# Fifteen instead of eleven pairs of value units as seven block products, in a two-layer hybrid decoder trunk

## The reference

```python
eidx = jnp.take_along_axis(cidx, pos, axis=-1)          # 16 of 16384 experts for each of 8 heads
g = jax.nn.softmax(sc, axis=-1)
act = jax.nn.gelu(jnp.einsum('bchkd,bcd->bchk', u[eidx], hb).astype(jnp.float32))
return jnp.einsum('bchk,bchkd->bcd', (g * act).astype(hb.dtype), v[eidx])
```

## Time and profile before

| | |
|---|---|
| time, median of 3 runs | 2419.32 us (2418.03 to 2420.98) |
| time of the profiled execution | 2415.21 us |
| its span, first to last instruction | 2413.4 us |
| mean granted clock of TensorE | 0.999 |
| PE busy | 2386.7 us, 99% |
| PEld (weight loads) busy | 2215.5 us, 92% |
| DVE busy | 1885.1 us, 78% |
| ACT busy | 1437.1 us, 60% |
| POOL busy | 790.1 us, 33% |

### The profile page before, as it was taken

The page is one execution under the profiler, slowest core; times in us unless marked ns, Lnnn a source line. Parts: engine busy times, 40 slices in busy tenths (PEclk is TensorE's granted clock), DMA queues, the critical chain, the costliest instruction groups (busy, mean ns, idle before and its releaser), DMA issues.

```text
span 2413.4 us, 43665 instructions
## 1 busy us (share of the span) xinstructions
PE 2386.7 (99%) x17465; PEld 2215.5 (92%) x17465; DVE 1885.1 (78%) x3186; ACT 1437.1 (60%) x2115; POOL 790.1 (33%) x452
## 2 busy tenths in 40 slices
PE   9999999999999999999999999999999999999999
PEld 8999999999999988888799999999999999888887
DVE  7988777498489975888778886865974899768886
ACT  5586664444677764655455966644446777555553
POOL 0011410288899820000000113003888988100000
PEclk9999999999999999999999999999999999999999
DMA  7533345355544455666555333453555444566654
GB/s 262 215 123 123 122 141 189 135 184 185 177 162 160 158 201 192 211 208 214 183 186 207 133 123 112 152 185 137 184 184 175 158 160 162 196 198 211 200 183 157
DMA packets 103016, 419.26 MB, mean 174 GB/s; under 512 B 11552, under 2 KB 12064, under 8 KB 85920
## 3 DMA queue, kind: packets, MB, share of 16 engines
q1 hardware_dynamic: 102816, 416.47, 50.7%
HBM read 415.38 MB, written 1.05 MB: 173 GB/s over the span
## 4 chain that ended last, share of the span: by engine, by line
PE 85%; DVE 6%; ACT 3%; DMA 3%; issue 2%; POOL 1%; SPq 0%; DVEq 0%; ACTq 0%
PE banks L2278 20%; PE banks L407 18%; PE banks L408 18%; PE banks L409 18%; PE banks L2260 3%; DMA xr<-in_xstream 2%; PE banks L2294 1%; PE banks L2295 1%; PE banks L2293 1%; DVE ring_lo L382 1%; PE banks L867 1%; ACT xr_hi L1871 1%; DVE xr_lo L1876 1%; POOL xr_lo L1876 1%; PE banks L754 1%
## 5 line engine op out<-in xcount | busy, mean ns | idle before, releaser
L1871 ACT ACTIVATE xr_hi<-xr 128x1024 fp32r<-128x1024 f32 x468 | 493.8, 1056 | 437.7 <-DMA xr<-in_xstream 437.3
L1876 POOL TENSOR_TENSOR xr_lo<-xr,xr_hi 128x1024 fp32r<-128x1024 f32 x256 | 619.9, 2426 | 388.7 <-ACT xr_hi L1871 388.3
L407 PE MATMUL banks<-featH,xr_hi 128*128 128x256 f32 x2048 | 576.1, 281 | 1.1 <-POOL xr_lo L1876 1.1
L408 PE MATMUL banks<-featL,xr_hi 128*128 128x256 f32 x2048 | 575.7, 281 | 0.0
L409 PE MATMUL banks<-featH,xr_lo 128*128 128x256 f32 x2048 | 575.3, 281 | 0.0
L407 PEld LDWEIGHTS banks<-featH,xr_hi 128*128 128x128 f32 x2048 | 385.7, 188 | 1.9 <-POOL xr_lo L1876 1.0
L409 PEld LDWEIGHTS banks<-featH,xr_lo 128*128 128x128 f32 x2048 | 386.1, 189 | 0.0
L408 PEld LDWEIGHTS banks<-featL,xr_hi 128*128 128x128 f32 x2048 | 385.9, 188 | 0.0
L1876 DVE TENSOR_TENSOR xr_lo<-xr,xr_hi 128x1024 fp32r<-128x1024 f32 x212 | 259.3, 1223 | 159.1 <-ACT xr_hi L1871 157.9
L407 PE MATMUL banks<-featH,ring_hi 128*128 128x256 f32 x1232 | 351.0, 285 | 2.2 <-DVE ring_lo L382 1.5
L408 PE MATMUL banks<-featL,ring_hi 128*128 128x256 f32 x1232 | 346.2, 281 | 0.0
(11 more groups left out here) (416 smaller groups left out, 4629.9 us busy)
## 6 DMA issues: line engine op xcount, KB each, us to landing
xr<-in_xstream SPq DMA_DIRECT2D x468, 512.0 KB, 3.3
ring<-in_wstream SPq DMA_DIRECT2D x128, 1024.0 KB, 4.9
b_raw<-in_xstream SPq DMA_DIRECT2D x88, 256.0 KB, 3.6
smw<-in_small SPq DMA_DIRECT2D x4, 617.0 KB, 9.2
first<-in_wstream SPq DMA_DIRECT2D x4, 512.0 KB, 5.5
first<-in_wstream SPq DMA_DIRECT2D x2, 1024.0 KB, 7.9
subk<-in_subkeys SPq DMA_DIRECT2D x2, 1024.0 KB, 7.7
x<-in_x SPq DMA_DIRECT2D x2, 512.0 KB, 5.6
```

The source lines that it names most:

```text
L407: PE.matmul(o, s_hi_lo[0], m_hi_lo[0], start=first, stop=False)
L408: PE.matmul(o, s_hi_lo[0], m_hi_lo[1], start=False, stop=False)
L1871: A.activation(xr_hi[:, m % XR], xr[:, m % XR], ACT.Copy).then_inc(s_xhi, 1)
L1876: (PO if m < NKEY else V).tensor_tensor(xr_lo[:, m % XR], xr[:, m % XR], xr_hi[:, m % XR].bitcast(F32), ALU.subtract).then_inc(s_xlo_pool ...
```

## The change

`SEVEN` names 15 pairs instead of 11. The first three stay where they were (7, 15, 23); behind them the pairs are alternately three and two apart instead of four. The sevens then stand ahead of plain units 14, 28, 42, 46, 48, 52, 54, 58, 60, 64, 66, 70, 72, 76 and 78 of 98. Between two of them lie 4 or 2 plain units, where 6 lay before. The steps in `lead` are set anew, so that for the alternating sevens the first sums stand two units ahead of the seven before, the last sums, `sums_high` and `b_low` one unit ahead of it, and all the rest at it. For the first three sevens `b_low`, `a_high`, `a_sums` and `a_sums_high` come one step later. Four loads of the second buffer set are issued in two steps instead of four, and the next layer's first splits stand at units 120 and 124 (ACT) and 122 and 126 (DVE). The loads of the next layer are tied to the last sevens and move with them.

```diff
--- before.py
+++ after.py
@@ -110,8 +110,8 @@
-SEVEN = (7, 15, 23, 27, 31, 35, 39, 43, 47, 51, 55)
-SEVEN_SET = (0, 0, 0, 1, 0, 1, 0, 1, 0, 1, 0)
+SEVEN = (7, 15, 23, 26, 28, 31, 33, 36, 38, 41, 43, 46, 48, 51, 53)
+SEVEN_SET = (0, 0, 0, 1, 0, 1, 0, 1, 0, 1, 0, 1, 0, 1, 0)
 PLAIN = tuple(i for i in range(NKEY) if i // 2 not in SEVEN)
 ONE_BY_ONE = len(PLAIN)
 SEVEN_AT = tuple(2 * r - 2 * j for j, r in enumerate(SEVEN))
@@ -2098,17 +2098,17 @@
                 OTHER_FREE = sum(i < 42 for i in PLAIN)
                 OTHER_AFTER = sum(2 * r < 42 for r in SEVEN)
-                def lead(j, units, later=0):
-                    return SEVEN_AT[j] - units if SHARED[j] else SEVEN_AT[j - 1] - 1 + later
-                B_HIGH = FIRST_SUMS = tuple(lead(j, 11) for j in range(NS))
-                LAST_SUMS = tuple(lead(j, 10) for j in range(NS))
-                SUMS_HIGH = B_LOW = tuple(lead(j, 9, 1) for j in range(NS))
-                A_HIGH = A_SUMS = tuple(lead(j, 8, 1) for j in range(NS))
-                A_SUMS_HIGH = tuple(lead(j, 7, 1) for j in range(NS))
-                SUMS_LOW = tuple(lead(j, 6, 1) for j in range(NS))
-                A_LOW = tuple(lead(j, 4, 3) for j in range(NS))
+                def lead(j, units, later):
+                    return SEVEN_AT[j] - units if SHARED[j] else SEVEN_AT[j - 1] + later
+                B_HIGH = FIRST_SUMS = tuple(lead(j, 11, -2) for j in range(NS))
+                LAST_SUMS = tuple(lead(j, 10, -1) for j in range(NS))
+                SUMS_HIGH = tuple(lead(j, 9, -1) for j in range(NS))
+                B_LOW = tuple(lead(j, 8, -1) for j in range(NS))
+                A_HIGH = A_SUMS = tuple(lead(j, 7, 0) for j in range(NS))
+                A_SUMS_HIGH = SUMS_LOW = tuple(lead(j, 6, 0) for j in range(NS))
+                A_LOW = tuple(lead(j, 4, 0) for j in range(NS))
                 def one_by_one(unit):
@@ -2198,10 +2198,11 @@
                             sp.wait_ge(s_xu, past(s_xu) + VU + done)
                             for piece in range(2 * done - 2, 2 * done):
                                 b_load(0, piece)
-                        if OTHER_FREE <= done < OTHER_FREE + 4:
+                        if done in (OTHER_FREE, OTHER_FREE + 1):
                             sp.wait_ge(s_xu, past(s_xu) + VU + OTHER_FREE)
                             sp.wait_ge(s_bmul, past(s_bmul) + OTHER_AFTER)
-                            b_load(SEVEN_SET.index(1), done - OTHER_FREE)
+                            for piece in range(2 * (done - OTHER_FREE), 2 * (done - OTHER_FREE) + 2):
+                                b_load(SEVEN_SET.index(1), piece)
                         if done in SEVEN_AT:
                             j = SEVEN_AT.index(done)
                             if layer + 1 < L:
@@ -2411,8 +2412,8 @@
                     for i in range(ONE_BY_ONE):
                         if i and i % 2 == 0:
                             p_hi_pair(i // 2 + 1)
-                        if layer + 1 < L and i in (one_by_one(116), one_by_one(120)):
-                            programs[layer + 1]["split_hi"](act, i // one_by_one(120))
+                        if layer + 1 < L and i in (one_by_one(120), one_by_one(124)):
+                            programs[layer + 1]["split_hi"](act, i // one_by_one(124))
                         x_hi(act, VU + i + XR - 1)
                         for j in range(NS):
                             if i == B_HIGH[j]:
@@ -2655,8 +2656,8 @@
                     for i in range(ONE_BY_ONE):
                         if i and i % 2 == 0:
                             p_lo_pair(i // 2 + 1)
-                        if layer + 1 < L and i in (one_by_one(119), one_by_one(123)):
-                            programs[layer + 1]["split_lo"](dve, i // one_by_one(123))
+                        if layer + 1 < L and i in (one_by_one(122), one_by_one(126)):
+                            programs[layer + 1]["split_lo"](dve, i // one_by_one(126))
                         if i + XR - 1 < ONE_BY_ONE:
                             x_lo(dve, VU + i + XR - 1)
                         for j in range(NS):
```

## The result

The changed kernel takes **2496.1 us** (median of 6 runs, 2493.7 to 2501.4) beside 2420.15 us for the kernel before, measured along with it: ratio 1.0317, 95% interval 1.0307 to 1.0327. That is 76 us slower, in the direction forecast, but 33 us over the predicted 2463 us and beyond the range's end at 2484. In the changed kernel's profile all lines from L2204 on have a number one higher than before.

The account below looks back on a forecast made before the run. PE's own work was taken to bound the value stage. The profiled 2415.2 + 51.6 (12 new waits) - 4.7 - 1.0 - 1.8 = 2459.3 us, beside the median 2463 us, 1.8% slower; range 2446 to 2484.

Parts of the forecast that it names:

- rival 4: Sevens four units behind another are late too, as raw blocks land late: 2 to 3 us each, 2490 us; chance 5%.
- the chain from `xr_lo` on: Preparation of a seven two units behind another, from DVE's split of its unit to the last `a_low`: 11.7 us.
- The length of the waits: PE's wait ahead of each of 12 sevens two units behind another: 17.2 us chain against PE's 13.0, so 4.2 us.
- The first link: From unit 50's end to ACT's `xr_hi` of unit 54, through its load: 4.4 us, then 1.09 to `xr_lo`.
- a restart costs some 0.1 more: PE's first matmuls behind each of the 12 waits: 0.1 us added, making 4.3 us each, 51.6 us in all.
- Rival 1: PE's clock falls in the 12 new waits: 13 to 26 us more, about 2480 us; chance 11%.
- The gain on PE: Four more pairs as sevens in each of two layers, 0.59 us saved per pair: 4.7 us less.
- DVE's sum: DVE's work per two sevens and six units, 26.2 us against PE's 26.0; hidden inside a period of 30.3 us.
- The late splits: At the first layer's end two PE waits go, 2.4 us, with 0.6 charged at the last: 1.8 us less.
- The first three sevens: `acts_lo` comes out earlier because `b_low` moves a step later: 1.0 us less for both layers.
- Rival 2: DVE's idle time hides the preparation and the gain comes: 2412 us, or 2414 with DVE's excess; chance 10%.
- rival 3: `sums_high` doesn't hold up `p_hi` and `xr_hi`, DVE's order bounds: waits of 3.1 us, 2449 us; chance 8%.

Follow-up runs that it names:

- `fill`: The changed kernel with 18 matmuls of zeros ahead of PE's wait at each of the 12 short-gap sevens: 2472.6 us, ratio 1.0215.
- `early2_sums`: The changed kernel with the short-gap sevens' whole preparation two steps earlier and ACT's `sums_high` one step later: 2418.9 us, ratio 0.9998 against the kernel before.
- `sums_later`: The changed kernel with ACT's `sums_high` one step later, behind `p_hi` and the next split as before: 2480.5 us, ratio 1.0248 against the kernel before.
- `early2`: The changed kernel with the whole preparation of each short-gap seven two steps earlier on both engines: 2445.3 us, ratio 1.0102 against the kernel before.
- `threes`: The changed kernel with 13 sevens, three pairs apart behind the first three, and `sums_high` one step later: 2416.15 us, ratio 0.9987 against the kernel before.

## Why the prediction came out as it did

- **That PE waits, where, how often and for what**: right. Twelve waits, at units 48 to 78 of each layer, for `a_sum_lo`; no wait at the four-unit sevens (rival 4 falls), and the chain from `xr_lo` on within 0.1 us.
- **The length of the waits**: 4.2 us taken, 4.57 us on average measured (54.9 / 12). The mean lies inside the ends of 3.4 and 5.6, single waits on both sides of them (3.24 to 6.21). The first link was short, in the seven at 54 by 0.6 us: it was sized from two instances of 4.28 and 4.51 where the earlier trace rows had landings up to 5.4 us, and neither taking ACT's part out of its way nor both parts made the mean clearly shorter.
- **What stands behind each wait: "a restart costs some 0.1 more", and nothing for the clock**: this is the step that failed. The restart itself was sized rightly (`fill`: 0.11 us each). But the 0.1 us, read off waits of about 1 us, stood in the sum for all that follows a wait of 4 us. The clock was a term of zero in it. What came was 26.0 us over 12 waits, 2.2 each, and `fill` shows that 24.6 us of it are the clock's. Rival 1 described it properly, priced it at 13 to 26 us and got 11%, although the forecast itself put PE at rest for 4 us twelve times. It should have been a term of the forecast: 2463 plus its 13 to 26 is 2476 to 2489. "PE is wholly busy between the waits", the argument against, turned out to be no protection: 1000 to 1020 us is at 1.00 with PE busy all of it, and 1026.6 to 1031 at 0.50. The argument for it was also stated too weakly: 4.2 us is over three times the longest wait of PE in the stage before, 1.28 us, and not twice. The Trainium skill (TensorE: Matmul & The Clock Gate, section Why this matters for your kernels) warns of idle gaps between bursts of matmuls. These rows bear the warning out. The absence of such a stretch in the trace of before was no evidence against it, since that trace had no such gap to show.
- **The gain on PE**: 4.7 taken; by the rows 5.0. The prediction took every seven at 4.85 us, and half of the new ones, those of set 1, take 4.76.
- **DVE's sum, 26.2 against PE's 26.0 us**: right, and it decides what a repair can bring. `early2_sums` has every chain in time and comes out even, with a period of 26.6 us.
- **The late splits**: 1.8 taken, 2.2 measured alone (0 to 4.4), with the waits at the end of the stage as foretold. **The first three sevens**: 1.0 us less taken, 1.9 more measured (its bound was 1 more). The 4.3 us of the earlier trace rows, from which the gain was argued, end at 1160 us and so leave out the layer's end, which the prediction counted in.
- **Rival 2 (the chain is hidden)** falls with the 12 waits; **rival 3** falls in the changed kernel, and `sums_later` shows what letting the split past would have been worth.

By terms, the 33 us are: the slow clock and restarts 26.0 - 1.2 = 24.8; the idle times 54.9 - 50.4 = 4.5; the first three sevens 1.9 + 1.0 = 2.9; and 0.3 and 0.4 less for PE's gain and the late splits. Together 31.5. Another 0.8 is the kernel before itself, 2420.15 us beside the changed kernel where the prediction had 2419.3.

Left open: why some loads land later than others, and so why single waits reach 5.67 and 6.21 us. No run separates the load's neighbours on the DMA engines. Open too is what decides whether the clock falls behind a short wait: of the eight of 1.8 to 1.9 us in `early2` four were followed by a fall.

## What to carry to other kernels

A wait of PE can have two prices, its length and the slow matmuls behind it; when a forecast holds waits longer than any that the trace has, what follows them can't be read off the short ones, and a clock fall belongs in the sum as a term and not among the rivals. Walk the chain through the in-order queues of *all* engines, with its first link sized from many instances of the load and not from two. Before sevens (or whatever saves the bound engine work at another's expense) are added, compare the two engines' sums per period: where they are even, the saving has nowhere to go (`early2_sums`), and where the helper has room, it arrives, small as it is (`threes`).

## What the runs showed of the hardware

- After each of the 12 waits of 3.24 to 6.21 us, on an engine that was otherwise busy, TensorE ran at 1.2 GHz for a time: 128x512 matmuls 0.43 us apart instead of 0.23. In the shortest wait's case the slow pace only began with the fifth matmul behind the wait (granted clock 1.00 from 1122.50 to 1125.70 us, 0.51 from 1126.80 to 1130.10), so the first matmul's duration (0.50 us and not 0.80) doesn't tell whether the clock will fall; one has to read on.
- Shorter waits did it too: one of 2.30 us in `sums_later`, and four of eight of 1.83 to 1.86 us in `early2`. Behind the 12 waits of 0.18 to 1.69 us in `fill`, with matmuls of zeros ahead of them, the clock stayed at 1.00.
- Matmuls of zeros whose result nobody reads kept the clock: 18 of them per wait brought the stage from 0.95 to 1.00, and the kernel from 2496.1 to 2472.6 us, with the sevens held up by the same chain.
- The same reordering of `sums_high` was worth 15.6 us where the chain behind a load bound (the changed kernel), and 26 us where DVE's own sum did (`early2`).
